# First four column units of a hybrid decoder step: computed side by side by quarters of the depth, with x and weights loaded in turn

## The reference, cut to what matters

```python
def rmsnorm(x, g):
    y = x * lax.rsqrt(jnp.mean(x * x, axis=-1, keepdims=True) + RMS_EPS)
    return y * g
n = rmsnorm(x, norm1)                 # x: 288 tokens x 2048
c_rw, c_att, c_gate = split(n @ w_in) # 48 column tiles of 128, then the gates
```

## Time and profile before

| | |
|---|---|
| median of 3 runs | 1846.82 us (1845.8 to 1849.24) |
| span of the profiled execution | 1844.8 us, 2.0 us less than the median |
| TensorE matmul busy | 1811.2 us, 98% of the span |
| VectorE busy | 1132.4 us, 61% |
| ScalarE busy | 729.2 us, 40% |
| GpSimd busy | 51.6 us, 3% |
| moved by DMA | 283.52 MB, mean 154 GB/s |

### The profile page before, as it was taken

One profiled execution on the slowest core, in us unless ns is written; L12 is line 12 of the kernel. 1 busy time (PEld: TensorE's weight loads), 2 busy tenths in 40 slices (PEclk: granted clock), 3 DMA queues, 4 the chain that ended last, 5 costly groups with the idle time before them and its releaser, 6 DMA issues.

```text
span 1844.8 us, 41091 instructions
## 1 busy us (share of the span) xinstructions
PE 1811.2 (98%) x16688; PEld 1733.0 (94%) x16688; DVE 1132.4 (61%) x2000; ACT 729.2 (40%) x1013; POOL 51.6 (3%) x100
## 2 busy tenths in 40 slices
PE   7999999999999999999999999999999999999997
PEld 6999788888888888899999999999999999999997
DVE  6645675467777777766556666666666665434444
ACT  5433434344444444433444333333333333333332
POOL 0600000000000000000000000000000000000000
PEclk9999999999999999999999999999999999999999
DMA  6644334333333332355446444544445445544443
GB/s 238 223 160 158 108 115 160 119 128 109 107 107 107 107 102 91 130 199 166 167 170 219 160 162 161 177 160 159 161 163 176 159 159 184 188 163 166 161 167 129
DMA packets 50832, 283.52 MB, mean 154 GB/s; under 512 B 7104, under 2 KB 12288, under 8 KB 24656
## 3 DMA queue, kind: packets, MB, share of 16 engines
q1 hardware_dynamic: 43488, 260.80, 41.6%
q10 hardware_dynamic: 3216, 12.82, 1.8%
q0 software_dynamic: 4064, 8.98, 1.5%
HBM read 274.31 MB, written 8.27 MB: 153 GB/s over the span
## 4 chain that ended last, share of the span: by engine, by line
PE 94%; DVE 3%; ACT 1%; DMA 1%; issue 1%; SPq 0%; ACTq 0%; DVEq 0%
PE bank L596 29%; PE bank L598 27%; PE bank L597 27%; PE bank L925 1%; PE bank L960 1%; DVE w_lo L544 1%; PE bank L612 1%; PE bank L1025 0%; PE bank L947 0%; DVE max L1813 0%; PE bank L577 0%; PE bank L725 0%; PE bank L882 0%; PE bank L701 0%; PE bank L791 0%
## 5 line engine op out<-in xcount | busy, mean ns | idle before, releaser
L596 PE MATMUL bank<-x_split,w_lo 128*128 128x288 f32 x2944 | 899.3, 305 | 7.1 <-DVE w_lo L544 6.9
L597 PE MATMUL bank<-x_split,w_hi 128*128 128x288 f32 x2944 | 869.2, 295 | 0.0
L598 PE MATMUL bank<-x_split,w_hi 128*128 128x288 f32 x2944 | 867.0, 294 | 0.0
L560 ACT ACTIVATE w_hi<-w_raw 128x2048 fp32r<-128x2048 f32 (+1 forms) x262 | 468.8, 1790 | 590.4 <-PE bank L598 571.7
L544 DVE TENSOR_TENSOR w_lo<-w_raw,w_hi 128x2048 fp32r<-128x2048 f32 (+1 forms) x238 | 503.6, 2116 | 283.8 <-ACT w_hi L560 283.5
L596 PEld LDWEIGHTS bank<-x_split,w_lo 128*128 128x128 f32 x2944 | 552.4, 188 | 32.1 <-issue 13.6
L597 PEld LDWEIGHTS bank<-x_split,w_hi 128*128 128x128 f32 x2944 | 553.8, 188 | 3.1 <-issue 0.7
L598 PEld LDWEIGHTS bank<-x_split,w_hi 128*128 128x128 f32 x2944 | 554.9, 188 | 0.0
L596 PE MATMUL bank<-act_split,w_lo 128*128 128x288 f32 x704 | 208.6, 296 | 0.0
L597 PE MATMUL bank<-act_split,w_hi 128*128 128x288 f32 x704 | 207.7, 295 | 0.0
L598 PE MATMUL bank<-act_split,w_hi 128*128 128x288 f32 x704 | 207.0, 294 | 0.0
(11 more groups left out here) (384 smaller groups left out, 1499.9 us busy)
## 6 DMA issues: line engine op xcount, KB each, us to landing
w_raw<-in_w_up SPq DMA_DIRECT2D x88, 1024.0 KB, 4.8
w_raw<-in_w_in SPq DMA_DIRECT2D x48, 1024.0 KB, 5.0
w_raw<-in_w_down SPq DMA_DIRECT2D x64, 704.0 KB, 4.1
w_raw<-in_w_gate SPq DMA_DIRECT2D x32, 1024.0 KB, 4.9
w_raw<-in_w_p SPq DMA_DIRECT2D x16, 1024.0 KB, 4.9
w_raw<-in_w_o SPq DMA_DIRECT2D x16, 1024.0 KB, 4.8
x_raw<-in_x SPq DMA_DIRECT2D x4, 576.0 KB, 5.7
h<-in_x ACTq DMA_DIRECT2D x1, 2304.0 KB, 11.1
```

Of the source, the lines that this page charges most:

```text
L560: actv(WHI[:, slot, 0:kt], WRAW[:, slot, 0:kt], ACT.Copy).then_inc(sem("w_hi"), 3 if isinstance(n, int) and n == 2 else 1)
L596: mm(out, wl, hi, start=first and k == ks[0], stop=False, skip_group_check=True)
L597: mm(out, w, lo, start=False, stop=False, skip_group_check=True)
L598: ins = mm(out, w, hi, start=False, stop=last and k == ks[-1], skip_group_check=True)
```

## The change

- SP's queue: x is loaded in five parts (2, 2, 4, 4 and 4 tiles), and the first two weight slots between them. The first quarter of slot 0 (256 KB) is issued by ACT's queue, ahead of its two parameter loads. The main constants come after the load of slot use 2 instead of 1.
- The weights of units 0 to 3 are laid out anew in memory: load s (0 to 3) holds the depth's quarter s of all four units, and not one unit.
- PE: `first_units` goes through the quarters s of the depth, and in each through units 0 to 3, with four tiles of depth for each unit; each unit has a bank of its own (2 to 5). The eight sums ahead of unit 0 and the two in it become one sum (bank 6), between units 1 and 2 of the last quarter.
- ACT and DVE: x's high and low parts are signalled tile by tile; weights and x are split in turn. DVE adds all the squares to one tile. An activation that loads ACT's table runs as soon as the gains have landed; another loads the root's table ahead of the root.
- The root comes after the last quarter has begun, and the four banks are multiplied by it one after the other. `SWAP` becomes 7 and `FIRST_ROPE` 10.

```diff
-SWAP = 4
-FIRST_ROPE = 7
+FIRST = 4
+SWAP = 7
+FIRST_ROPE = 10
...
+            load_x(0, 2, "x_in0")
+            load_x(2, 4, "x_in0b")
+            sp.dma_start(WRAW[:, 0, 4:KT, :]..., a["w_in"][0][:, 4 * P:]).then_inc(sem("w_in0"), 16)
+            load_x(4, 8, "x_in1")
+            sp.dma_start(WRAW[:, 1, :, :]..., a["w_in"][1]).then_inc(sem("w_in1"), 16)
+            load_x(8, 12, "x_in2")
+            load_x(12, 16, "x_in3")
...
-            pe.wait_ge(sem("x_split"), 1)
-            first_sums(range(0, 4), 3)
-            first_sums(range(4, 8), 6)
+            def first_units():
+                for s in range(4):
+                    slot = s % 2
+                    for u in range(FIRST):
+                        if s < 2 and u < 3:
+                            pe.wait_ge(sem("w_part"), 3 * s + u + 1)
+                        else:
+                            pe.wait_ge(sem("w_split"), s + 1)
+                        out = BK[first_bank(u)][:, 0:N]
+                        for k in range(4):
+                            t = 4 * s + k
+                            if u == 0:
+                                pe.wait_ge(sem("x_split"), t + 1)
+                            hi, lo, w, wl = XN[:, 0, t], XN[:, 1, t], WHI[:, slot, 4 * u + k], WLO[:, slot, 4 * u + k]
+                            mm(out, wl, hi, start=t == 0, ...)
+                            mm(out, w, lo, ...)
+                            ins = mm(out, w, hi, stop=t == KT - 1, ...)
+                        if u == FIRST - 1:
+                            ins.then_inc(sem("unit_done"), 1)
+                        if s == 3 and u == 1:
+                            first_sum()
...
-                    if n == 0 and q == 2:
-                        first_sums((8, 9), KT).then_inc(sem("norm_sq_used"), KT)
...
         @block.scalar
+            act.dma_start(WRAW[:, 0, 0:4, :]..., a["w_in"][0][:, 0:4 * P]).then_inc(sem("w_first_in"), 16)
...
             act.wait_ge(sem("norms_in"), 16)
+            actv(ROOT[:, 0:1], NORMS[:, 0, 0:1], ACT.Copy)
+            act.wait_ge(sem("w_first_in"), 16)
+            first_weights(0, [0])
+            first_hi(0, 2, "x_in0")
+            first_hi(2, 4, "x_in0b")
+            act.wait_ge(sem("w_in0"), 16)
+            first_weights(0, [1, 2, 3])
+            first_hi(4, 8, "x_in1")
             first_squares(0)
+            act.wait_ge(sem("w_in1"), 16)
+            first_weights(1, [0, 1, 2, 3])
+            first_hi(8, 12, "x_in2")
             first_squares(1)
+            split_hi(act, 2, 0)
+            first_hi(12, 16, "x_in3")
             first_squares(2)
             first_squares(3)
+            split_hi(act, 3, 1)
+            split_hi(act, 4, 0)
+            actv(ROOT[:, 0:1], MEANS[:, 0:1], ACT.Sqrt)
...
         @block.vector
+            first_weights(0, [0])
+            first_lo(0, 4)
+            first_weights(0, [1, 2, 3])
+            first_lo(4, 8)
+            first_weights(1, [0, 1, 2, 3])
+            first_lo(8, 12)
+            split_lo(dve, 2, 0)
+            add_quarter(1)
+            first_lo(12, 16)
+            split_lo(dve, 3, 1)
+            add_quarter(2)
+            add_quarter(3)
+            st.done(V.tensor_tensor(SQ[:, 0:2, :], SQ[:, 0:2, :], SQ[:, 2:4, :], ALU.add))
+            V.tensor_tensor(SQ[:, 0, :], SQ[:, 0, :], SQ[:, 1, :], ALU.add).then_inc(sem("norm_sq"), 4)
+            split_lo(dve, 4, 0)
             norm_rstd(0, RSTD)
...
+            for n in range(FIRST - 1):
+                scaled_out(n)
+            for n in range(FIRST - 1, FIRST_COLS):
                 if n <= SWAP:
                     scaled_out(n)
...
-                if n < 2:
-                    normed(2 * n)
-                    normed(2 * n + 1)
+                for i in {3: (0,), 4: (1, 2), 5: (3,)}.get(n, ()):
+                    normed(i)
...
+    first = arr["w_in"][:FIRST].reshape(FIRST, P, 4, KT // 4 * P)
+    arr["w_in"][:FIRST] = first.transpose(2, 1, 0, 3).reshape(FIRST, P, D_MODEL)
```

More of the change, by code:

```diff
@@ L495, in section @@
                 if u0 == 0:
-                    body(0)
+                    for n in range(2, per):
+                        load(n, n % 2, src[0, n], kt)
                     with sp.Fori(1, LATE_CACHE_GROUP) as g:
@@ L545, in split_lo, with first_bank @@
                              ALU.subtract).then_inc(sem("w_split"), 1)
+        def first_bank(n):
+            return 2 + n if n < FIRST else n % 2
         def split_part(dve, n, slot, part):
@@ L571, in settle, with first_sum @@
                 eng.sem_inc(sem("pe_step"), 1)
[L573 to L578, removed]
+            def first_sum():
+                pe.wait_ge(sem("norm_sq"), KT)
+                mm(BK[6][:, 0:N], mean_ones, SQ[:, 0, :], start=True, stop=True).then_inc(sem("norm_sq_used"), KT)
             def last_sum(k, total, squares):
@@ L619, in index_weights @@
                    stop=True).then_inc(sem("wi_rows"), 1)
-            for n in range(FIRST_COLS):
-                if n >= 2:
-                    pe.wait_ge(sem("w_split"), n + 1)
+            for n in range(FIRST, FIRST_COLS):
+                pe.wait_ge(sem("w_split"), n + 1)
+                if n >= FIRST + 2:
                     pe.wait_ge(sem("unit_out"), n - 1)
@@ L1249, in unit_out, with first_unit @@
                 actv(samples(tile[:, 1 + SEQ:E], 5), by_request(BK[j % 2][:, SEQ:N]), ACT.Copy).then_inc(sem("unit_out"), 1)
+            def first_unit(n):
+                act.wait_ge(sem("unit_done"), n + 1)
+                if n > SWAP:
+                    if n == SWAP + 1:
+                        act.wait_ge(sem("unit_out"), SWAP + 1)
+                    unit_out(COLS[:, FIRST_COLS + n, :], n % 2)
+                if n == SWAP:
+                    norm_hi(3)
+                split_hi(act, n + 2, n % 2)
+                if n == SWAP - 1:
+                    for i in range(3):
+                        norm_hi(i)
             def in_units(g):
                 for j in range(4):
[L1253 to L1275, removed]
+                    act.wait_ge(sem("unit_done"), g * 4 + j + 1)
+                    unit_out(step(colsv[:, bass.ds(g + FIRST_COLS // 4, 1), j, :]), j)
+                    split_hi(act, g * 4 + j + 2, j % 2)
+            for n in range(FIRST - 1, 12):
+                first_unit(n)
+            with act.Fori(3, FIRST_COLS // 4) as g:
                 in_units(g)
```

110 lines of the change are left out of this document (50 added, 60 removed).

## The result

The changed kernel takes 1869.8 us (median of four runs, 1856.85 to 1877.46) against 1846.7 (four runs, 1845.8 to 1849.24): a ratio of 1.0123 [1.0099, 1.0147]. The forecast was 1837.3, faster. The runs of before lie within 0.2% of each other, those of after within 1.1%. The profiled execution of after took 1856.85 us, the fastest of its runs, with a span of 1855.2. One execution of a kernel of experiment 5 took 2165.1 us at a granted clock of 0.751, a slow one, and is left out of its figures.

A forecast was written before the change was run, and what follows sets the result against it. PE, busy 98% of the span, was taken as the bound. Four units ending at 35.6 instead of 45.1 gain 9.5 us: 1844.8 - 9.5 = 1835.3 of span, plus 2.0, gives 1837.3 us; range 1834.8 to 1841.3.

The forecast's parts named there:

- Start 6.8: Kernel's beginning: PE's first product of weights and x at 6.8 us instead of 18.56, bounds 6.0 to 8.5.
- low pace 5.4 us: PE's first 5.4 us of work run at half pace, now on weight products: cost 2.7 us, bounds 1.4 to 5.4.
- four units at 35.6: End of the first phase: PE has units 0 to 3 done at 35.6 us instead of 45.1.
- Gain 9.5: First phase: units 0 to 3 end 9.5 us sooner, all of it taken off the whole span.
- Quarter 2's supply (21.6) takes back all beyond 0.7: Ahead of quarter 2: weights ready at 21.6 for PE at 22.3, so faster start or clock gains only 0.7 us.
- Everything from there on runs in the same order afterwards, at intervals set by PE.: All behind the first four units: order and PE's intervals stay, so the early gain reaches the end whole.
- semaphore counts by tile cost nothing visible: First phase: signalling x's parts tile by tile was taken to add no visible time.
- A: Rival: VectorE becomes the bound at quarter 2 and unit 5, costing 2 to 4 us; 1839.5 to 1842; chance 0.13.
- B: Rival: early start pays nothing, as a load that doesn't move stops PE later; 1846.8, no change; chance 0.05.
- C: Rival: waits for tiles and parts in quarters 0 to 3 keep PE's low pace; 13.9 us slower, 1860.7; chance 0.04.
- D: Rival: w's first quarter lands only at 8.2, PE starts at 9.3, 2.5 us less gain; 1839.8; chance 0.09.
- 0.03 for something slower that wasn't listed: Remaining chance, 0.03, given to an unnamed slower outcome anywhere in the kernel.

The follow-up runs named there:

- experiment 5: Changed kernel with unread matmuls ahead of PE's first product to work off the low pace, plus variants of squares and load order; medians 1835.6 to 1837.6 us.
- +57: Changed kernel with 14 unread matmuls of ones (56 PE instructions) and a wait for their input at PE's head; 1836.2 us, ratio 0.9948.

## Why the prediction was wrong, point by point

**Right: the account of the phase.** Start 6.8 (was 7.22), low pace 5.4 us (5.4), quarter 2 at 22.3 (22.54), its weights at 21.6 (22.16, so 0.4 to spare for 0.7), quarter 3 at 28.7 (28.94), four units at 35.6 (35.81), reciprocal to 36.4 (36.83), `w_lo` of unit 5 at 41.1 (41.16) for 42.0 (42.21). Gain 9.5 (9.4). One pair of sum matmuls is left, and the table was loaded by 3.7. The additions for the sum come to 31.3 by the forecast's own terms and not to 31.2 (31.80 in after, for a PE that wanted them near 32.1). With the loop in a good place all of it reaches the end: 1837.3 us. That the low pace lasted 5.4 us in before and in after is in part luck: with the same products first it lasted 4.7 us in the kernel with 36 increments, 3.3 in the one with the early load and 36 increments, and 4.0 to 4.5 in the other four. In the kernel with 36 increments PE and `w_lo` were ready for quarter 2 together, at 22.06 (it began at 22.11), so that a low pace shorter still would have gained nothing.

**Right, and in the main shown by taking it away: supply comes next.** "Quarter 2's supply (21.6) takes back all beyond 0.7": the kernels that worked off the low pace gained nothing measurable, and PE waited for `w_lo` ahead of quarter 2 for 0.2 us with 14 warm products and 0.8 with ten. Their later first products (8.81 and 8.19) took back a part as well.

**Wrong: "Everything from there on runs in the same order afterwards, at intervals set by PE."** The order is the same, and the intervals are not. The sentence looks at work and waits, and leaves out that code itself has to be fetched. The nine sums that were taken out, costed at nothing beyond their path, and "semaphore counts by tile cost nothing visible" are right as times. As instructions they are 40 places in PE's stream: of the two states of the pair loop, seven blocks or eight, they chose the worse. Its price is the 32.5 us between after (1869.8) and the same kernel with 36 increments (1837.3); less the 9.4 gained early, that is the measured +23.

The trace of before had enough to list this as a rival: 47 packets on queue 8, none of them in the loop. By the count, 30 of 256 places are bad ones (256 - 226), so for a change that shifts the loop by an arbitrary number it deserves about 0.12, at 5 to 8 us for each repeat, 30 to 50 here. A count of PE's instructions would have put the loop just beyond the edge (231 for 225), close enough to be a rival with a large chance.

**The rivals.** A: no stop on DVE in after; its margins held. B: nothing that PE reaches sooner stopped it for want of data; only its outcome, a phase 9.4 us shorter and a span that isn't, is near, with another mechanism. C: the low pace ended at 12.63, and waits for tiles inside the units did not bring it back. D: the first weights came in time (landed at 5.04 for 5.6). What happened is the 0.03 for something slower that wasn't listed, and the range, built from terms inside the first 45 us alone, couldn't hold it.

**Open.** Why at after's own place only three of six rounds (five of six with the increments behind the loop) are slow, while eight instructions further on all are. With the loop ending some six instructions into its eighth block, the load of the next and the branch back are 0.2 us apart, so a race of the two is likely, but no run was made for it. The edge itself was only bracketed: bad at 0, +8 and +24, good at +36, +40 and +57. That neighbours of the first block are lost one after the other, which makes nine packets a round, is read from the times of the loads.

**The versions to keep.** The change with 36 increments ahead (1837.3, 0.9948 [0.9936, 0.996]) and that with warm products and late squares (1835.6, 0.9943 [0.9931, 0.9956]) both beat before and after; their intervals overlap, so they can't be told from each other.

## What to carry to other kernels

An edit ahead of a long loop moves the loop in the engine's instruction stream. Where a loop's instructions nearly fill what the engine holds (here 1567 in blocks of 256), count how many blocks it touches before and after the edit, and compare the packets on the instruction queue inside the loop: none is good, nine a round is a bill of 5 to 8 us each. If an unchanged loop becomes slower, with waits put down to "issue", shift it by a few dozen empty instructions under a wait that is there anyway before blaming the change.

## What the runs showed of the hardware that was not expected

- A loop on PE repeats with no instruction load at seven blocks, and at eight it reloads itself, in every round with eight or 24 increments and in three or five of six at after's place: 47.4 us a round against 52.5 to 56.5, with PE idle for 4.5 us (after) to some 6.9 (24 increments).
- That idle time costs clock on top. With 24 increments PE is at the lower level (1.2 GHz) for 6.8 us behind the wait in five of the six rounds and for 10.2 in the last; the first has a mean granted clock of 0.94, the last of 0.91. The first 8 us behind the first such wait, a window of that kernel:

```profile
450.00:458.00 8.00, 7.27 (x146) 6.52 (x145) 2.19 (x9) 2.60 (x9) 0.00 (x0) 0.68 0.01 4
```

  The Trainium skill (TensorE: Matmul & The Clock Gate, HAM oscillation) has waits between groups of matmuls bring the throttle back, and here the trace agrees; the shorter waits of after's second round (1.67 and 2.80 us) left it at 1.00.
- A row of semaphore increments on PE takes about 0.16 us each (232 in 36.9).
- In the first 5.4 us of PE's work the pace is half, 0.24 us for 0.13, in both kernels, while the windows give a clock of 1.00. The traces hold no record of the clock before 17.20 us in before and 12.75 in after, when the pace has just risen, and a stretch without a record reads full. The low level at the start is seen in the pace alone.
